# Layer 1's first output-projection block issued between the attention pairs, with one PSUM bank set aside

## What is computed

```python
h = rms_norm(x, norm_mix[layer])
y_mix, xq = fox_group(h, w_in_b[j], b_forget[j], fox_q_gain[j], fox_k_gain[j])   # (512, 512)
y_mem = memory_group(xq, mem, ...)                                               # (512, 512)
x = x + jnp.concatenate([y_mix, y_mem], axis=-1) @ w_out[layer]                  # 1024 -> 1024
x = x + sqrelu_mlp(rms_norm(x, norm_mlp[layer]), w_mlp_in[layer], w_mlp_out[layer])

def one_block(args):                 # inside fox_group, one block of 128 queries, 8 heads of 64
    s = jnp.einsum("bhqd,bhkd->bhqk", qb, kh).astype(jnp.float32) * scale
    s = s + cb[..., :, None] - c[:, :, None, :]          # forget gates, summed
    s = jnp.where(pos[:, None] >= k_pos[None, :], s, NEG_INF)
    p = jax.nn.softmax(s, axis=-1)
    return jnp.einsum("bhqk,bhkd->bhqd", p.astype(vh.dtype), vh)
```

## Time and profile before

| | |
|---|---|
| runs | 2796.48, 2796.89, 2805.78 us |
| profiled execution | 2802.87 us, span 2801.3 us, mean granted clock 0.987 |
| TensorE busy | 2711.2 us, 97% |
| VectorE busy | 1593.4 us, 57% |
| ScalarE busy | 990.4 us, 35% |
| forget-gate attention | from 720.37 us to 770.43 us of the span |

### The profile page before, as it was taken

One profiled execution on the slowest core, in us unless ns is written; L12 is line 12 of the kernel. 1 busy time (PEld: TensorE's weight loads), 2 busy tenths in 40 slices (PEclk: granted clock), 3 DMA queues, 4 the chain that ended last, 5 costly groups with the idle time before them and its releaser, 6 DMA issues.

```text
span 2801.3 us, 45290 instructions
## 1 busy us (share of the span) xinstructions
PE 2711.2 (97%) x19179; PEld 2250.6 (80%) x19179; DVE 1593.4 (57%) x2330; ACT 990.4 (35%) x1363; POOL 194.0 (7%) x272
## 2 busy tenths in 40 slices
PE   8989999999899999999999999999989999999998
PEld 6778888888688888777878888888768878888887
DVE  5567777755667777765554553333585454633334
ACT  5653222244632222353332431223433433432223
POOL 5000000000000000001050000000010130000000
PEclk9999999999999999999999999999999999999999
DMA  4233555522035555320023323232220023223231
GB/s 157 91 113 125 184 169 171 170 76 76 1 115 183 176 162 172 100 91 27 4 80 95 101 90 106 91 106 79 75 65 8 25 89 99 91 91 105 91 101 65
DMA packets 238828, 281.15 MB, mean 100 GB/s; under 512 B 9646, under 2 KB 225202, under 8 KB 238642
## 3 DMA queue, kind: packets, MB, share of 16 engines
q1 hardware_dynamic: 225322, 226.28, 25.2%
q0 software_dynamic: 13184, 52.11, 6.3%
q10 hardware_dynamic: 136, 0.03, 0.0%
HBM read 276.30 MB, written 2.10 MB: 99 GB/s over the span
## 4 chain that ended last, share of the span: by engine, by line
PE 89%; DVE 6%; ACT 3%; issue 2%; DMA 0%; ACTq 0%; DVEq 0%; POOL 0%; POOLq 0%
PE psum L2512 25%; PE psum L2513 24%; PE psum L2514 24%; DVE wlo L1618 1%; PE psum L2586 1%; PE psum L2588 1%; PE psum L2587 1%; PE psum L3051 1%; PE psum L3066 1%; ACT whi L908 1%; PE psum L3034 1%; PE psum L3090 1%; PE psum L3023 0%; PE psum L2981 0%; PE psum L2999 0%
## 5 line engine op out<-in xcount | busy, mean ns | idle before, releaser
L2512 PE MATMUL psum<-hh,whi 128*128 128x512 f32 (+1 forms) x2032 | 789.5, 389 | 9.3 <-DVE wlo L1618 6.2
L2513 PE MATMUL psum<-hl,whi 128*128 128x512 f32 (+1 forms) x2032 | 779.9, 384 | 0.0
L2514 PE MATMUL psum<-hh,wlo 128*128 128x512 f32 (+1 forms) x2032 | 779.9, 384 | 0.0
L1618 DVE TENSOR_TENSOR wlo<-raw,whi 128x2048 fp32r<-128x2048 f32 x219 | 503.1, 2298 | 478.7 <-ACT whi L908 478.3
L908 ACT ACTIVATE whi<-raw 128x2048 fp32r<-128x2048 f32 x219 | 418.3, 1910 | 526.5 <-PE psum L2514 522.2
L2512 PE MATMUL psum<-mh,whi 128*128 128x512 f32 (+1 forms) x1248 | 487.5, 391 | 7.5 <-DVE wlo L1618 4.3
L2513 PE MATMUL psum<-ml,whi 128*128 128x512 f32 (+1 forms) x1248 | 480.9, 385 | 0.0
L2514 PE MATMUL psum<-mh,wlo 128*128 128x512 f32 (+1 forms) x1248 | 480.8, 385 | 0.0
L2512 PEld LDWEIGHTS psum<-hh,whi 128*128 128x128 f32 x2032 | 383.5, 189 | 98.0 <-issue 11.6
L2514 PEld LDWEIGHTS psum<-hh,wlo 128*128 128x128 f32 x2032 | 383.3, 189 | 75.6
L2513 PEld LDWEIGHTS psum<-hl,whi 128*128 128x128 f32 x2032 | 383.9, 189 | 73.5 <-issue 0.5
(11 more groups left out here) (468 smaller groups left out, 2731.4 us busy)
## 6 DMA issues: line engine op xcount, KB each, us to landing
rest<-in_ada_w POOLq DMA_DIRECT2D x64, 768.0 KB, 5.3
raw<-in_w_gu SPq DMA_DIRECT2D x44, 1024.0 KB, 5.1
raw<-in_w_in SPq DMA_DIRECT2D x34, 1024.0 KB, 5.2
raw<-in_w_mlp_in SPq DMA_DIRECT2D x32, 1024.0 KB, 5.4
raw<-in_w_mlp_out SPq DMA_DIRECT2D x32, 1024.0 KB, 5.0
raw<-in_w_out SPq DMA_DIRECT2D x16, 1024.0 KB, 5.0
raw<-in_w_down SPq DMA_DIRECT2D x16, 1024.0 KB, 5.0
raw<-in_w_mem_kv SPq DMA_DIRECT2D x8, 1024.0 KB, 5.0
```

Source lines behind the costliest of these rows:

```text
L1618: ins = dve.tensor_tensor(wlo[:, g % 2, :, :], raw[:, g % 2, :, :], f32(whi[:, g % 2, :, :]), ALU.subtract)
L2512: pe.matmul(out, whi_, xhi, start=first, stop=False)
L2513: pe.matmul(out, whi_, xlo, start=False, stop=False)
L2514: return pe.matmul(out, wlo_, xhi, start=False, stop=last)
```

## The change

The plan keeps one bank from the ring during the 16 pairs, and gives it back once block 0 of slab 0 is listed. The first block's k steps 4 and 5 are issued in turn 8, 6 and 7 in turn 12, 0 and 1 in turn 16, each piece between the scores and the transposes of its turn (there are no scores in turn 16). After the loop, block 1 runs its first six k steps alone, then both blocks take k = 2 and k = 3. Slabs 1 to 3, and layer 0, stay as they were.

```diff
             if l:
+                self.keep_bank()
                 self.attend_pairs(l)
-            self.lin("wo", l, 4)
+                self.block("wo", l, 0, 0, kept=True)
+                self.give_bank()
+                self.block("wo", l, 0, 1)
+                for s in range(1, 4):
+                    self.slab_jobs("wo", l, s, 2)
+            else:
+                self.lin("wo", l, 4)
...
+                    def mixed_ready(k):
+                        evacuated(pe, J["xa_o", l, 2 * (k - 4) + 1] if k >= 4 else J["fox_o", l, NT * (k + 1) - 1])
+                    def out_part(p, b, k):
+                        g = plan.slab["wo", l, 0]
+                        w = (slice(0, P), g % 2, k, slice(b * P, (b + 1) * P))
+                        return three(p, whi[w], wlo[w], mh[:, k, :], ml[:, k, :], k == 4, k == 3)
+                    def out_ahead(ks):
+                        pe.wait_ge(raw_used, plan.slab["wo", l, 0] + 1)
+                        p = ahead("wo", l, 0, 0)
+                        for k in ks:
+                            mixed_ready(k)
+                            out_part(p, 0, k)
+                    def out_rest():
+                        p = ahead("wo", l, 0, 1)
+                        for k in (4, 5, 6, 7, 0, 1):
+                            mixed_ready(k)
+                            out_part(p, 1, k)
+                        mixed_ready(2)
+                        out_part(bank(J["wo", l, 0, 0]), 0, 2)
+                        out_part(p, 1, 2)
+                        mixed_ready(3)
+                        done(out_part(start("wo", l, 0, 0), 0, 3))
+                        done(out_part(start("wo", l, 0, 1), 1, 3))
...
                             if j < PAIRS:
                                 fox_scores(j)
+                            if j in (8, 12, 16):
+                                out_ahead({8: (4, 5), 12: (6, 7), 16: (0, 1)}[j])
...
-                for s in range(4):
-                    linear("wo", l, s, y, before=mixer_out if s == 0 else None, first=4 * l)
+                if l:
+                    out_rest()
+                for s in range(l, 4):
+                    linear("wo", l, s, y, before=mixer_out if s == 0 else None)
```

More of the change, by code:

```diff
@@ L2894, in mixer_out @@
                         evacuated(pe, J["xa_o", l, 2 * (k - 4) + 1])
-                    elif l == 0:
+                    else:
                         pe.wait_ge(S("lru_lo"), k + 1)
-                    else:
-                        evacuated(pe, J["fox_o", l, NT * (k + 1) - 1])
-                for s in range(4):
-                    linear("wo", l, s, y, before=mixer_out if s == 0 else None, first=4 * l)
+                if l:
+                    out_rest()
+                for s in range(l, 4):
+                    linear("wo", l, s, y, before=mixer_out if s == 0 else None)
                 def mlp1(cc, c):
```

## The result

The changed kernel took 2814.88 us (median of four runs, 2811.34 to 2818.1) against 2798.86 us for four runs of the kernel before: ratio 1.0048, 95% interval 1.0033 to 1.0064. By the ratio it is slower by 13 us, with 9 and 18 as ends; the two medians of four runs lie 16.0 us apart. The forecast was 11.4 us slower. The kernel before, run 23 more times beside the first experiments, has a median of 2802.04 us, so the 2796.89 us from which the forecast counted was a low sample.

The account below looks back on a forecast made before the run. TensorE, busy 97% of the span, was taken as the bound. Stage +12.0 us, less 4.1 behind it, gave +7.9; +3.5 for lower clock made +11.4, from 2796.89 to 2808.3 us, range 2797 to 2820.

Parts of the forecast that it names:

- Which bank waits for whom: Forget-gate attention, layer 1: with seven banks, scores of pair j wait for pair j-5's values' low part; transposes lose theirs.
- The ring's price: Serial loop from one pair's scores to the next: 3.39 to 4.76 us a pair, 16.16 us per four, against 10.66.
- The pieces: Projection matmuls moved into the attention loop, 1.36 us a piece: turns 8 and 12 add 1.55 us, turn 16 adds 0.3.
- Given back behind the attention: 18 projection matmuls are gone behind the attention: -4.1 us, really given back since what lies behind keeps up.
- The clock: TensorE at its lower clock level for four to five pairs of the attention: +3.5 us, bounds -1.7 and +12.
- at full clock: Attention stage +12.0 us (scores 15 later by 11.7, third piece 0.3, tail kept), less 4.1 us behind it: +7.9 us.
- The sum: Whole kernel: +7.9 us without clock loss, +3.5 us for lower clock: +11.4 us, 2808.3 us from the 2796.89 us median.
- The rule on the clock: TensorE idling briefly while cycling through PSUM banks can swing between clocks, losing throughput; alone, it implies the upper bound, +12.
- the pieces fill the idle places: Rival: moved matmuls fill TensorE's attention stalls and the bank wait hardly shows: 2789 to 2793 us; chance 10%.
- The gaps don't compound: Rival: each pair starts late by its own gap and catches up, stage grows by 2.4 us: about 2799 us; 10%.
- Half clock for nearly the whole stage: Rival: each of eleven attention pairs pays some 0.8 us, pieces 2.7 us: 2813 to 2817, up to 2822 us; 25%.

Follow-up runs that it names:

- run 23: Not a label but a count: the kernel before, unchanged, was timed 23 more times beside the first experiments; median 2802.04 us.
- the early release: Values' high and low parts taken at the head of the turn: in the changed kernel, 2794.53 us; in the kernel before (eight banks, no pieces), 2797.8 us.

## Why the prediction was right

- **Which bank waits for whom**: right for the pairs. The wait stands in front of the scores and names the values' low part; six banks cost the same as seven; the bank alone brings the whole slowdown. Wrong for turn 16: the prediction said that no wait for the bank is left in front of the transposes, and 0.45 us of it stands there (0.79 us without the piece).
- **The ring's price**: right, a little low. Scores 5 to 15 took 43.9 us, 41.9 forecast. From the low part's start to TensorE's start it is 0.43 us (747.07 to 747.50), not the 0.35 taken from rows 3 and 5, which is 0.8 to 0.9 us over the ten steps; another 0.9 is the fall of the clock in turn 12 (5.27 us against 4.36), and 0.2 are the pieces of turns 8 and 12.
- **The pieces**: right for turns 8 and 12. Turn 8 took 4.36 us, forecast 4.16; without a piece 3.49 (744.68 to 748.17, the experiment with the bank alone), so a piece costs 0.87 us of the ring, in the middle of the bounds. The 0.3 us of turn 16 is right by luck. From scores 15 on the changed kernel took 8.78 us, against 8.46 and 8.48 in the two later profiles of the kernel before, which is 0.3; but with the bank set aside and no piece it took 8.78 us as well. So the third piece cost nothing, and the 0.3 us is the wait for the bank.
- **Given back behind the attention**: right, 4.07 us.
- **The clock**: the mis-sized term. The forecast put +3.5 us of lower clock on top; the two profiles of the changed kernel are at 62.9 us with some 0.9 us of it. Besides, the sum called "at full clock" kept a tail of 9.75 us that ran in part at half clock, and the changed kernel's did not, which is 1.3 us less. Against the base profile the term was about -0.4 us. (Its reading of rows 2 stops short, too: TensorE idled on to 739.64 us, so 1.34 us of idle time stood right ahead of the first fall, not 0.6.)
- **The sum**: that 11.4 us still lies inside the measured 9 to 18 is luck in part: the ring is 1 us dearer, the base profile's stage was 1.3 us longer than the mean of three, and 3 to 4 us between the medians come from outside the stage, unsettled. From the median of 2802.04 us the same sum gives 2813.4 us.
- **The rule on the clock**: the rule named from the Trainium skill (TensorE: Matmul & The Clock Gate, "A second HAM failure mode: psum-queue depth-cycling") fits best the kernel that sets the bank aside from turn 8 on, where swings to the lower level cost 6 us in the first profile and 5 us in the second, by an estimate from the turns' lengths; in the two kernels with the early release the clock did not fall in the stage at all.
- **The rivals**: "the pieces fill the idle places" is what happens with the early release (2794.53 us); in the change its condition, no wait in front of the scores, was not met. "The gaps don't compound" fell: 1.3 us at pair 5 had become 13.9 us at pair 15 (54.2 us into the stage, 40.3 before). "Half clock for nearly the whole stage" fell too (0.97 on the mean), although the measured median lies inside its 2813 to 2817 us: both counted from 2796.89 us.

## What to carry to other kernels

Before a buffer is taken out of a ring, write down for each job which one it will wait for, and in which instruction's shadow the release stands; if the release is queued behind work that needs the waiting job's predecessor, the loop runs in series, here with seven banks and with six alike. The cheapest repair was two instructions moved to the head of their turn. Filler work pays only where it stands in the queue ahead of the instruction that waits, so that it runs during the wait; in the change the wait had moved in front of the scores, and the pieces stood behind them.

## What the runs showed of the hardware

The clock often fell in this stage, and idle time just ahead does not foretell it. In both profiles of the kernel that takes the bank from turn 8 on it was at its lower level in turns 8 and 12; a turn with six 512-column matmuls then took 6.85 us instead of 4.36. In both profiles of the changed kernel, with the same 2.4 us of idle time ahead of scores 8 and 12, it stayed up in turn 8 and fell in the middle of turn 12. With the bank alone set aside it fell ahead of turn 12 and stayed low through turn 13. With the banks handed out by kind it was low from 726 to 740 us, behind idle times in the stage of at most 1.10 us. In the two kernels with the early release it stayed at its upper level for the whole stage, in one of them with an idle time of 1.35 us in turn 16. What tells these apart is open; all but three of the kernels have a single profile.

One profile is a thin base for a stage like this: three of the kernel before differ by 2.6 us over 50, by the clock alone.
